# Seven products for eight in three sections of the last block, and the first weight tile ahead of x

## What is computed

```
h = rmsnorm(x, g_pre)
proj = h @ w_in              # 1024 -> 12 parts of 512 + 4 gates of 1024
out_a = gmlp_spatial(a_u, layernorm(a_v)) * silu(a_z)
out_b = silu(layernorm(conv31(b_a * sigmoid(b_b)))) * silu(b_z)
out_c = multiscale_pool(c_x) * silu(c_z)
out_d = d_b * conv3(d_c * d_x) * silu(d_z)
gates = sigmoid(gate_logits + b_gate)
merged = sum over 4 branches of gates[b] * (out_b @ w_branch[b])
x = x + rmsnorm(merged @ w_out, g_post)
```

## Time and profile before

| | us |
|---|---|
| median of 3 runs | 2459.53 (2459.49 to 2459.98) |
| profiled execution | 2460.2 |
| its span | 2458.1 |
| TensorE busy | 2434.8 |
| VectorE busy | 1258.1 |
| ScalarE busy | 393.5 |
| GpSimd busy | 329.2 |

### The profile page before, as it was taken

The page is one execution under the profiler, slowest core; times in us unless marked ns, Lnnn a source line. Parts: engine busy times, 40 slices in busy tenths (PEclk is TensorE's granted clock), DMA queues, the critical chain, the costliest instruction groups (busy, mean ns, idle before and its releaser), DMA issues.

```text
span 2458.1 us, 34054 instructions
## 1 busy us (share of the span) xinstructions
PE 2434.8 (99%) x12772; PEld 2116.8 (86%) x12772; DVE 1258.1 (51%) x1923; ACT 393.5 (16%) x602; POOL 329.2 (13%) x173
## 2 busy tenths in 40 slices
PE   9999999999999999999999999999999999999998
PEld 7888887788888888888888888888899999999997
DVE  6776878752535455643344455654144545554323
ACT  5222222323011000111101000010201100000101
POOL 5435444444000000001000000000200000000000
PEclk9999999999999999999999999999999999999999
DMA  8868887787644555555654555555554344444457
GB/s 320 313 240 298 299 297 283 256 291 268 242 177 171 205 202 207 207 180 205 250 194 163 200 198 217 185 197 197 211 199 156 131 168 177 149 165 171 151 181 280
DMA packets 120382, 528.57 MB, mean 215 GB/s; under 512 B 11664, under 2 KB 14096, under 8 KB 74192
## 3 DMA queue, kind: packets, MB, share of 16 engines
q1 hardware_dynamic: 106032, 502.21, 57.1%
q10 hardware_dynamic: 14240, 24.89, 2.8%
HBM read 409.02 MB, written 118.03 MB: 214 GB/s over the span
## 4 chain that ended last, share of the span: by engine, by line
PE 96%; DVE 2%; issue 1%; DVEq 0%; POOL 0%; DMA 0%; ACT 0%; POOLq 0%; ACTq 0%
PE acc L1231 82%; PE acc L1474 6%; PE side L1369 4%; PE acc L1334 1%; PE side L1396 1%; PE side L1386 1%; PE side L1256 0%; DVE cb L791 0%; PE acc L1375 0%; PE side L1277 0%; DVE tmp L1026 0%; POOL w_pair L402 0%; DMA col<-in_cols 0%; DVE sq_y L1124 0%; DVE merged L1029 0%
## 5 line engine op out<-in xcount | busy, mean ns | idle before, releaser
L1231 PE MATMUL acc<-h_hi,w_pair 128*128 128x512 f32 (+1 forms) x5984 | 1553.3, 353 | 0.0
L1231 PEld LDWEIGHTS acc<-h_hi,w_pair 128*128 128x128 f32 x5984 | 1027.0, 188 | 142.3 <-issue 3.6
L1231 PE MATMUL acc<-h_lo,w_pair 128*128 128x512 f32 (+1 forms) x2992 | 951.4, 351 | 0.0
L1231 PEld LDWEIGHTS acc<-h_lo,w_pair 128*128 128x128 f32 x2992 | 529.3, 188 | 72.2 <-issue 3.6
L791 DVE SCALAR_TENSOR_TENSOR cb<-glu,col,cb 128x512 f32<-128x512 f32 x600 | 396.1, 725 | 23.2 <-issue 18.6
L1231 PE MATMUL acc<-out_hi,w_pair 128*128 128x512 f32 (+1 forms) x1280 | 346.5, 352 | 5.0 <-DVE tmp L1026 5.0
L402 POOL TENSOR_TENSOR w_pair<-w_raw,w_pair 128x512 fp32r<-128x512 f32 (+1 forms) x119 | 272.2, 2299 | 278.5 <-ACT w_pair L500 264.8
L1231 PEld LDWEIGHTS acc<-out_hi,w_pair 128*128 128x128 f32 x1280 | 221.3, 188 | 36.1 <-DVE tmp L1026 6.3
L1026 DVE TENSOR_TENSOR tmp<-acc,sig 128x512 f32<-128x512 f32 (+1 forms) x96 | 68.0, 708 | 342.2 <-PE acc L1231 340.3
L416 POOL TENSOR_TENSOR rstd<-msq,nhalf 128x5 f32<-128x5 f32 (+3 forms) x18 | 19.1, 1063 | 1648.0 <-DVE msq L725 797.7
L510 ACT ACTIVATE sig<-acc,col 128x512 f32<-128x512 f32 (+1 forms) x128 | 90.0, 703 | 896.3 <-PE acc L1231 894.3
(11 more groups left out here) (173 smaller groups left out, 1458.9 us busy)
## 6 DMA issues: line engine op xcount, KB each, us to landing
w_pair<-split_main SPq DMA_DIRECT2D x272, 1024.0 KB, 4.8
split_main<-w_pair SPq DMA_DIRECT2D x88, 1024.0 KB, 6.5
w_pair<-split_branch SPq DMA_DIRECT2D x96, 512.0 KB, 3.7
w_raw<-in_w_main SPq DMA_DIRECT2D x88, 512.0 KB, 5.1
split_branch<-w_pair SPq DMA_DIRECT2D x32, 512.0 KB, 6.5
w_raw<-in_w_branch SPq DMA_DIRECT2D x32, 256.0 KB, 5.6
xr<-in_x_t ACTq DMA_DIRECT2D x3, 2048.0 KB, 13.2
out_y_t<-xr ACTq DMA_DIRECT2D x6, 1024.0 KB, 7.7
```

What stands on the lines that cost most here:

```text
L1231: ins = pe.matmul(acc[:, s, b, 0:m], wt[slot][:, wk], mv_[:, k, t0:t0 + m], start=(k == 0 and n == 0), stop=(k == nk - 1 and n == 2))
```

## The change

**Seven for eight.** In D, G1 and G3 of the last block two weight tiles (256 output columns) are taken together with both halves of 288 tokens as a 2 x 2 by 2 x 2 block product, and done as seven products of 512 rows by 128 columns by 288 tokens instead of eight. Each product is 4 x 3 = 12 matmuls (`product`). The seven use sums of weight blocks (s1 to s4) and of input blocks (t1 to t4), and are put together from the PSUM banks with additions (`pair_sums`). D has eight such pairs, G1 and G3 four each; after each pair of G1 and G3 follow its two branch units.

**Sums of weights.** The four sums of each of the 16 pairs are made in blocks 1 and 2, eight pairs in each, from loop body 4 on (bodies of four units; body 8 is the second of G0). `s_load` reads two raw tiles, POOL makes the sums, ACT casts them behind the third unit of the body (`s_cast`), POOL makes the low parts, and SP stores both in `s_store`, two transfers of 1 MB, ahead of the load for the third unit of the next body.

**Sums of inputs.** `t_steps` on DVE and `t_cast` on ACT make them in the last block's G0.

**Weights in the last block.** In the three sections the ring is eight chunks of 0.5 MB, one to a product or a branch unit (`load_chunk`). `skipped` corrects the counts of the semaphores for what the ring did not load.

**Convolution.** In the last block 8 of its steps stand after B instead of 4, and 4 in D instead of 8.

**Start.** The first weight tile is loaded ahead of x, its cast is ahead of those of x, its low part is on DVE (`w_low`) instead of POOL, and there are 20 small matmuls, eight of them behind the cast. The waits of SP for x are gone, and `col` is loaded ahead of `ident`.

**Code.** Loops on SP and ACT in blocks 1 to 3 and on DVE in block 3 are written out.

The diff, cut to its core:

```diff
+SEVEN = ["D", "G1", "G3"]
...
+    def s_pair(j, it):
+        n = (it - 4) // 2
+        if 0 < j < NBLK - 1 and it >= 4 and n < NPAIR // 2:
+            return (j - 1) * (NPAIR // 2) + n, (it - 4) % 2
+        return None, None
...
-        for b in range(KT // 2):
-            sp.dma_start(xr[:, 2 * b:2 * b + 2, 0:BLK], x_t[:, 2 * b:2 * b + 2, 0:BLK]).then_inc(x_loaded[b], 16)
-            if b == 0:
-                raw_load(0, 0, raw_rows(MAIN0["B"]), DM)
-        for b in range(KT // 2 - 1):
-            sp.wait_ge(x_loaded[b], 16)
+        raw_load(0, 0, raw_rows(MAIN0["B"]), DM)
+        load_x(sp, 0)
...
+        def s_load(q):
+            if q == 0:
+                sp.wait_ge(w_lo_done, UPB)
+            else:
+                sp.wait_ge(s_stored, 32 * q)
+            for t in range(2):
+                sp.dma_start(w_raw[t][:, :], raw_rows(PAIR_TILE[q] + t)).then_inc(s_loaded, 16)
+        def s_store(q):
+            sp.wait_ge(s_lo_done, 2 * q + 2)
+            for n, part in enumerate((s_hi, s_lo)):
+                sp.dma_start(s_parts[q, :, n, :], f(part)).then_inc(s_stored, 16)
...
+        def load_chunk(name, n, src):
+            u0 = (NBLK - 1) * UPB + UNIT0[name]
+            slot = n % CHUNKS
+            if n - CHUNKS >= (0 if name == "G1" else CHUNK0[name]):
+                sp.wait_ge(chunk_done, n - CHUNKS + 1)
+            else:
+                sp.wait_ge(acc_done, u0 - RING + slot // 2 + 1)
+            sp.dma_start(f(chunk[slot]), src).then_inc(chunk_landed[slot], 16)
...
+                    q, phase = s_pair(j, UNIT0[name] // 4 + i)
                     for r in range(4):
                         u = u0 + i * 4 + r
+                        if phase == 0 and r == 0:
+                            s_load(q)
+                        if phase == 1 and r == 2:
+                            s_store(q)
...
+        def s_pair_sums(q):
...
+            pool.tensor_tensor(s1, a21, a22, ALU.add)
+            pool.tensor_tensor(s3, a11, a21, ALU.subtract)
+            pool.drain()
+            pool.tensor_tensor(s2, s1, a11, ALU.subtract)
+            pool.drain()
+            pool.tensor_tensor(s4, a12, s2, ALU.subtract)
+            pool.drain().then_inc(s_summed, 1)
+            for t in range(2):
+                pool.wait_ge(s_hi_done, 2 * q + t + 1)
+                pool.tensor_tensor(s_lo[:, t * DM:(t + 1) * DM], w_raw[2 + t][:, :], f(s_hi)[:, t * DM:(t + 1) * DM],
+                                   ALU.subtract).then_inc(s_lo_done, 1)
         powers = [0]
...
+        def s_cast(j, it, r):
+            q, phase = s_pair(j, it)
+            if phase == 0 and r == 2:
+                act.wait_ge(s_summed, q + 1)
+                for t in range(2):
+                    act.activation(s_hi[:, t * DM:(t + 1) * DM], w_raw[2 + t][:, :], ACT.Copy).then_inc(s_hi_done, 1)
...
+        def copy_p1(name, p):
+            if p and (name == "D" or p == PAIR0["G1"]):
+                act.wait_ge(pair_used, 2 * p)
+            elif p > PAIR0[name]:
+                act.wait_ge(pair_sig, sigs_before(name, p))
+            act.wait_ge(chunk_done, chunks_before(name, p) + 1)
+            act.activation(c22, banks(name, p)[0], ACT.Copy).then_inc(p1_copied, 1)
...
-        for dst, src in [(ident[:, :], ident_in), (col[:, :], cols)]:
+        for dst, src in [(col[:, :], cols), (ident[:, :], ident_in)]:
...
+        hi(0, 0, DM)
...
+        def w_low(u):
+            dve.wait_ge(w_hi_done, u + 1)
+            dve.tensor_tensor(w_lo[u][:, :], w_raw[u][:, :], f(w_hi[u]), ALU.subtract).then_inc(w_lo_done, 1)
...
-            for t in range(4):
+            for t in range(8 if last else 4):
...
+                        if last and ph == 0:
+                            t_steps(m)
...
+                def low(n, at):
+                    dve.wait_ge(t_hi_done, at)
+                    dve.tensor_tensor(t_lo[n][:, :, :], t[n], f(t_hi[n])[:, :, :], ALU.subtract).then_inc(t_lo_done, 1)
...
+                elif m == 6:
+                    low(4, 3)
+                else:
+                    low(3, 4)
+                dve.drain()
...
+            def pair_sums(name, p):
+                n = chunks_before(name, p)
+                bank = banks(name, p)
+                dve.wait_ge(p1_copied, p + 1)
+                dve.wait_ge(chunk_done, n + 2)
+                dve.tensor_tensor(c12, bank[1], c22, ALU.add).then_inc(pair_summed, 1)
+                dve.wait_ge(chunk_done, n + 3)
+                dve.drain()
+                dve.tensor_tensor(c21, bank[2], c12, ALU.add).then_inc(pair_summed, 1)
+                dve.wait_ge(chunk_done, n + 5)
+                dve.tensor_tensor(c11, bank[0], c22, ALU.add)
+                dve.drain()
+                dve.tensor_tensor(c12, bank[3], c12, ALU.add)
+                dve.tensor_tensor(c22, bank[3], c21, ALU.add).then_inc(pair_summed, 2)
+                dve.wait_ge(chunk_done, n + 6)
+                dve.drain()
+                dve.tensor_tensor(c12, bank[1], c12, ALU.add).then_inc(pair_summed, 1)
+                dve.wait_ge(chunk_done, n + 7)
+                dve.tensor_tensor(c21, bank[2], c21, ALU.add).then_inc(pair_summed, 1)
...
+            def section_done(n_sig):
+                dve.drain().then_inc(acc_done, 16)
+                for s in range(2):
+                    dve.drain().then_inc(acc_free[s], 8)
+                dve.drain().then_inc(sig_used, n_sig)
...
+                    for t in range(2):
+                        m = 2 * (p - PAIR0[name]) + t
+                        if conv_at is not None:
+                            conv_step(j, m + conv_at)
+                        dve.wait_ge(chunk_done, chunks_before(name, p) + 8 + t)
+                        dve.wait_ge(pair_sig, sigs_before(name, p) + 1 + t)
+                        dve.drain()
+                        dve.tensor_tensor(tv(tmp, j), branch_bank(m), tv(sig[t], j), ALU.mult).then_inc(pair_used, 1)
+                        dve.drain()
+                        dve.tensor_tensor(merged[:, m, :], merged[:, m, :], tmp[:, :], ALU.add)
+                        dve.drain()
+                        if ph == 3:
+                            split_merged(m)
+                section_done(8)
...
+            def seven_d(i):
...
+                p = PAIR0["D"] + 2 * i
...
+                pair_sums("D", p)
+                dve.drain()
+                dve.tensor_tensor(e[:, SH:SH + BLK], zc[0][:, 0:BLK], zc[1][:, 0:BLK], ALU.mult)
+                dve.tensor_tensor(e[:, 2 * SH + BLK:2 * SH + BLK + DEC], zc[0][:, BLK:WMAX], zc[1][:, BLK:WMAX], ALU.mult)
+                dve.drain().then_inc(pair_used, 2)
...
+                conv_step(j, 18 + i)
+                pair_sums("D", p + 1)
+                dve.drain()
+                dve.tensor_tensor(tmp[:, :], tmp[:, :], zc[0][:, :], ALU.mult)
+                dve.wait_ge(pair_sig, sigs_before("D", p + 1) + 1)
+                dve.drain()
+                dve.tensor_tensor(tmp[:, :], tmp[:, :], sig[0][:, :], ALU.mult)
+                dve.drain()
+                dve.tensor_tensor(tmp[:, :], tmp[:, :], zc[1][:, :], ALU.mult)
+                dve.drain().then_inc(pair_used, 2)
+                result(j, 0, i)
...
-        for _ in range(14):
+        for n in range(20):
+            if n == 12:
+                pe.wait_ge(w_hi_done, 1)
             pe.matmul(side[:, 1, 0:P], mean_mat[:, :], mean_mat[:, :], start=True, stop=True)
...
+            def product(n, rhs, bank):
+                landed(n)
+                wt = chunk[n % CHUNKS]
+                for k in range(CT):
+                    for c, (w_part, r_part) in enumerate(((0, 0), (0, 1), (1, 0))):
+                        ins = pe.matmul(bank, wt[:, w_part, k * P:(k + 1) * P], rhs[r_part][:, k, :],
+                                        start=(k == 0 and c == 0), stop=(k == CT - 1 and c == 2))
+                ins.then_inc(chunk_done, 1)
...
+            def seven(name):
...
+                if name != "G1":
+                    for s in range(2):
+                        pe.wait_ge(acc_free[s], u0 // 2)
+                if name == "D":
+                    pe.wait_ge(t_lo_done, 4)
...
+                for p in range(PAIR0[name], PAIR0[name] + n_pairs):
+                    n = chunks_before(name, p)
+                    bank = banks(name, p)
+                    first = p == PAIR0[name]
+                    if name == "D":
+                        if p >= 2:
+                            pe.wait_ge(pair_used, 2 * (p - 1))
+                    elif name == "G1" and first:
+                        pe.wait_ge(pair_used, 2 * p)
+                    elif not first:
+                        pe.wait_ge(pair_summed, 6 * p - 2)
+                    product(n, h11, bank[0])
+                    if gated_ and not first:
+                        pe.wait_ge(pair_summed, 6 * p - 1)
+                    product(n + 1, tt[2], bank[1])
+                    if gated_ and not first:
```

(51 more changed lines are left out.)

244 lines of the change are left out of this document (206 added, 38 removed).

## The result

The changed kernel takes **2535.74 us** (median of 6 runs), the kernel before 2460.09 (6 runs): ratio 1.031, 95% interval 1.0298 to 1.032. I predicted 2513 with a range to 2532: slower as forecast, and 23 us more than forecast, just outside the range. The profiled execution of the changed kernel took 2539.53 us, with a span of 2537.7, 79.6 more than before.

The account below looks back on a forecast made before the run. PE's matmuls were taken to bound the kernel, busy 2434.8 of 2458.1 us. 2460.2 - 25.6 + 21.6 + 0 + 47.2 + 13 - 2.7 = 2513.7 profiled, so 2513 us; range 2480 to 2532.

Parts of the forecast that it names:

- Seven products: D, G1 and G3 of the last block: 16 pairs go from 96 to 84 matmuls, -25.6 us.
- Seams: Last block's section changes and D's four bodies: PE waits 6.2, 3.2, 3.2, 5.0, 1.0 and 3.0, +21.6 us.
- Transfers of the last block: Last block: chunks keep up with products eating 328 GB/s, cost 0; bound +11 us at 282 GB/s.
- rival 2: D of the last block runs at the pace of its chunks: 2513 + 11 = 2524 us, chance 0.13.
- The stall of blocks 1 and 2: Blocks 1 and 2: weight load behind the two stores lands late and PE waits, 23.6 a block, +47.2 us.
- Rivals 3 and 4: Stores do not hold up the load, 2464 us, chance 0.06; only last block and start count, 2453, chance 0.08.
- The clock: Half clock behind eight new gaps of 5 us or more, in blocks 1, 2 and the last: +13 us.
- Rival 1: The clock stays, with no fall behind the new gaps: 2513 - 13 = 2500 us, chance 0.23.
- The discount: Only two thirds of 19.6 us taken for the eight gaps, because one case is thin: +13 us.
- the full term: Each of the eight gaps does what the one at the start did, losing 2.45 us: 19.6 us.
- The shorter gaps: Three gaps of at most 2.0 us before showed no fall, so gaps under 5 us got no clock cost.
- The start: Kernel's beginning: first unit starts earlier, first side job moves from 23.95 to 21.1, -2.7 us (0 to -4).

Follow-up runs that it names:

- the best kernel: The changed kernel with the cast behind the first unit, stores one load slot earlier, and last-block DVE work and waits reordered: 2438.78 us, ratio 0.9918.
- experiment 5: Compares the changed kernel with the best kernel, same 12592 PE instructions: the changed one is busy 36.2 us longer, 33.9 of it by the granted clock.
- the start alone: The kernel before with only the changed kernel's start (weight tile ahead of x, its low part on DVE, 20 small matmuls): 2460.84 us, ratio 1.0.

## Why the prediction was right and wrong, by its steps

- **Seven products**, -25.6: right. Between before and the best kernel busy time falls by 2434.8 - 2408.2 = 26.6. Of this 3.2 is before's own half clock (2.6 at the start, 0.6 more than the best kernel's at the very end), and six small matmuls cost the best kernel 1.0 (its small ones take 6.5 us, those of before 5.5): 26.6 - 3.2 + 1.0 = 24.4, which is 1.2 short of the forecast.
- **Seams**, +21.6: right. 6.2, 2.5, 3.3, 5.0 and 3.3 measured (20.3) against 6.2, 3.2, 3.2, 5.0 and 3.0; the last 1.0 of the sum is the slot at G3's start, in the next point. The five terms of a body of D add up to 8.1 and not to 8.2, which makes 2.4 and not 3.2. In the changed kernel's trace VectorE goes multiplication, 3.52 of convolution, 1.36 of low part, as priced.
- **Transfers of the last block**, 0: nearly. Within D the chunks never bind, at 288 GB/s from 2098 to 2200 us, so rival 2 is out. At G3's start two chunks are 2.7 late, where I had 1.0 for a free slot.
- **The stall of blocks 1 and 2**, +47.2: right, 48.9. In G sections 6.1 to 6.4 each (six), in D 3.4 and 4.5, from M to G0 2.5 and 1.4, from C to M none. Rivals 3 and 4 are out.
- **The clock**, +13: **this is the step that failed.** "The change makes eight gaps of 5 us or more ... so I take two thirds." It is 33.3 - 2.6 = 30.7 us by the 1-us stretches, or 36.2 - 3.2 = 33.0 by busy time, which holds 2.3 of other things (experiment 5); of the 25.8 us by which the profiled execution missed the sum, 18 to 20 lie here. Rival 1 is out. The step failed in two ways.
  - *The discount.* The eight gaps cost 19.1 together, almost the 19.6 of the full term; the discount had no row behind it.
  - *The shorter gaps.* Seven more falls, behind gaps of 1.8 to 4.5 us, cost 14.2. Five stand behind gaps that I had priced as idle time and given no clock (D to G1, G3 to O, body 11 twice, M to G0), one behind the start's 1.8 us, and one behind the 2.0 us at 444 us that the kernel before has as well.

  I had let the three gaps of at most 2.0 us stand for all shorter ones, and that reading was weak. The digits of the earlier trace rows cannot show a fall: the first slice has a 9 too, though the clock was 0.50 there from 10.5 to 15.5 us. The trace of before has indeed no fall behind these gaps, but that was one draw: the 2.0 us gap stands at the same place in all 13 traces of this case, and in 5 of them half clock follows it.

  "TensorE: Matmul & The Clock Gate" of the Trainium skill (section "Why this matters for your kernels") warns of idle gaps well shorter than 5 us too, so by its rule the term was not the whole 19.6 that I put beside it but more. With D to G1 (priced at 3.2) and body 11 (3.4, twice) among them, the price of the start's fall makes 11 x 2.45 = 27, much nearer to the 30.7.
- **The start**, -2.7: 2.3 at the first side job, and nothing that shows in the time. I stopped at a side job; behind it, in the trace of the start alone, the lead still met a fall that takes 1.7 us at 444 and a wait of 0.9 for a transfer at the end.

With the measured terms: -24.4 + 1.0 + 20.3 + 2.7 + 48.9 + 33.0 and -2.2 for the start's shorter gap make +79.3, against 79.6 by the spans. The median of the runs is 3.8 under the profiled execution, which was the slowest of the six. Its mean granted clock was 0.981, that of the four quickest 0.983: over the span this difference is some 5 us, so fewer falls can make up the 3.8. Only the profiled execution has a trace, so which falls were missing is not shown.

## What to carry to other kernels

In this kernel a gap of PE cost its length and, from 3.3 us on, about 2.2 us more at half clock, and no more behind 7.7 us (1.7) than behind 3.4 (1.7 and 2.8). So many gaps of 2 to 4 us are dearer than one long gap of the same sum, and a wait that cannot be removed is cheaper with throw-away matmuls in it. When a term rests on one gap that did nothing, look at it in more traces.

A store ahead of a load in one queue cost nothing here by its bytes alone, and 13.9 us by its wait alone, but 48.9 by both: the store's wait was released by the very unit whose end the load waits for, and the load then had 2 MB ahead of it. So before a wait is priced as given, ask which engine's order releases it: here one cast, moved by two units, was worth 68 us, and the reordered waits of the best kernel another 29.
